# Expert weights of a mixture-of-experts layer loaded as whole rows (16 KB in one piece), both column halves of a matrix together

## The reference

```python
SEQ, D_MODEL, N_EXPERTS, TOP_K, D_FF_2 = 256, 1024, 32, 4, 1024
# each of 256 tokens goes to 4 of 32 experts, y is the normed input of 256 x 1024
g = y @ w_gate_2[e] + b_gate_2[e]          # 1024 x 1024 for each expert
u = y @ w_up_2[e] + b_up_2[e]              # 1024 x 1024
g = minimum(g, 7.0); u = clip(u, -7.0, 7.0)
h = (u + 1) * g * sigmoid(1.702 * g)
out[token] += gate[token, e] * (h @ w_down_2[e] + b_down_2[e])   # 1024 x 1024
```

## Time and profile before

| | |
|---|---|
| median of 3 runs | 2488.28 us (2487.64 to 2488.79) |
| the profiled execution | 2488.91 us, of which the trace spans 2487.1 us |
| PE busy | 2242.4 us (90%) |
| PEld, DVE, ACT, POOL busy | 1451.0, 859.0, 568.9, 28.4 us |
| DMA | 594.04 MB, 239 GB/s on average over the span |
| chain that ended last, by engine | PE 66%, DMA 13%, SP's queue 10%, DVE 5%, issue 3%, ACT 2% |
| mean granted clock of TensorE | 0.955 of full speed |

### The profile page before, as it was taken

The page is one execution under the profiler, slowest core; times in us unless marked ns, Lnnn a source line. Parts: engine busy times, 40 slices in busy tenths (PEclk is TensorE's granted clock), DMA queues, the critical chain, the costliest instruction groups (busy, mean ns, idle before and its releaser), DMA issues.

```text
span 2487.1 us, 27199 instructions
## 1 busy us (share of the span) xinstructions
PE 2242.4 (90%) x11674; PEld 1451.0 (58%) x11674; DVE 859.0 (35%) x1503; ACT 568.9 (23%) x938; POOL 28.4 (1%) x61
## 2 busy tenths in 40 slices
PE   6998999998999999999998899888988898888981
PEld 3776878786875689998878433333333333333330
DVE  4244443523846667543655311111011111111101
ACT  3223332422424355433434200000000000000000
POOL 0000000000002100000000000000000000000000
PEclk8999999999999999999999899999999999999996
DMA  9533443324214445454206699999999999999990
GB/s 330 193 112 102 135 155 117 104 93 159 93 51 162 161 137 196 151 185 169 82 35 234 219 387 387 386 387 387 387 387 387 387 387 387 387 387 386 386 360 22
DMA packets 328288, 594.04 MB, mean 239 GB/s; under 512 B 6256, under 2 KB 78064, under 8 KB 327504
## 3 DMA queue, kind: packets, MB, share of 16 engines
q1 hardware_dynamic: 326240, 589.66, 65.7%
q10 hardware_dynamic: 1904, 2.31, 0.3%
HBM read 590.90 MB, written 1.05 MB: 238 GB/s over the span
## 4 chain that ended last, share of the span: by engine, by line
PE 66%; DMA 13%; SPq 10%; DVE 5%; issue 3%; ACT 2%; POOL 0%; DVEq 0%; ACTq 0%; POOLq 0%
PE ps L864 13%; PE ps L268 12%; PE ps L270 12%; PE ps L269 12%; DMA ring<-in_w_up_dram 12%; SPq L2019 10%; PE ps L835 2%; PE ps L852 2%; DVE wr L974 2%; PE ps L339 1%; PE ps L594 1%; PE ps L573 1%; PE ps L888 1%; DMA ring<-in_even_w_in_dram 1%; PE ps L580 1%
## 5 line engine op out<-in xcount | busy, mean ns | idle before, releaser
L864 PE MATMUL ps<-ring,big 128*64 128x512 f32 x3072 | 717.3, 623 | 108.1 <-DMA ring<-in_w_up_dram 66.1
L864 PEld LDWEIGHTS ps<-ring,big 128*64 128x64 f32 x3072 | 249.7, 143 | 550.1 <-issue 549.8
L268 PE MATMUL ps<-h_hi,wr 128*128 128x512 f32 (+1 forms) x960 | 341.8, 356 | 29.5 <-DVE h_lo L1026 25.3
L269 PE MATMUL ps<-h_lo,wr 128*128 128x512 f32 (+1 forms) x960 | 333.8, 348 | 0.0
L270 PE MATMUL ps<-h_hi,wr 128*128 128x512 f32 (+1 forms) x960 | 333.5, 347 | 0.0
L974 DVE TENSOR_TENSOR wr<-ring,wr 128x1024 fp32r<-128x1024 f32 (+1 forms) x248 | 283.7, 1203 | 132.9 <-ACT wr L1561 132.8
L1561 ACT CAST wr<-ring 128x1024 fp32r<-128x1024 f32 (+1 forms) x248 | 238.5, 1031 | 124.0 <-PE ps L270 101.5
L268 PEld LDWEIGHTS ps<-h_hi,wr 128*128 128x128 f32 x960 | 185.5, 193 | 61.5 <-issue 35.0
L269 PEld LDWEIGHTS ps<-h_lo,wr 128*128 128x128 f32 x960 | 185.6, 193 | 23.5 <-issue 2.9
L270 PEld LDWEIGHTS ps<-h_hi,wr 128*128 128x128 f32 x960 | 185.3, 193 | 21.8
L1435 DVE TENSOR_SCALAR hT<-ps 128x512 f32<-128x512 f32 x32 | 22.1, 692 | 334.9 <-PE ps L888 334.9
(11 more groups left out here) (288 smaller groups left out, 2616.8 us busy)
## 6 DMA issues: line engine op xcount, KB each, us to landing
ring<-in_w_gate_dram SPq DMA_DIRECT2D x64, 2048.0 KB, 19.7
ring<-in_w_up_dram SPq DMA_DIRECT2D x64, 2048.0 KB, 19.8
ring<-in_w_down_dram SPq DMA_DIRECT2D x64, 2048.0 KB, 19.9
ring<-in_ada_w_dram SPq DMA_DIRECT2D x24, 2048.0 KB, 10.9
ring<-in_ffn_w_up_dram SPq DMA_DIRECT2D x44, 1024.0 KB, 7.5
ring<-in_ffn_w_down_dram SPq DMA_DIRECT2D x16, 1408.0 KB, 6.1
ring<-in_w_in_dram SPq DMA_DIRECT2D x9, 2048.0 KB, 7.8
ring<-in_odd_w_qkv_dram SPq DMA_DIRECT2D x6, 2048.0 KB, 8.3
```

What stands on the lines that cost most here:

```text
L268: e.matmul(o, l[0], r[0], start=first, stop=False)
L269: e.matmul(o, l[0], r[1], start=False, stop=False)
L864: ins = e.matmul(pt[HALF[z], :], lhs[:, k, HALF[z]], wt[:, k, :], start=k == 0, stop=False, skip_group_check=True)
```

## The change

All 1024 columns of a matrix row are loaded together. Row 8p + k of a matrix goes to partition p, place k (`"(p k) n -> p (k n)"`), so that a partition's share of a load, four rows, is one piece of 16 KB. A load is still 2 MB and still half of one matrix of one expert, now the half k = 0 to 3 or k = 4 to 7 for every partition. Since the contraction index on partition p is now 8p + k and no longer 128k + p, the features of the other operand are permuted with it: `eighth(v, k)` takes every eighth column of `yN` or of the hidden activations, 128 of them 32 bytes apart, as the stationary operand.

`both` now fills two banks at once, and the couple is of k = 0 to 3 or k = 4 to 7 with both column halves. A pair does gate for both halves, two biases, up for both halves, two biases, then scatter, gather, both transposes, and down. Gate and up use the banks 4, 5 and 6, 7 in turn (`banks_of`). DVE multiplies sigmoid and gate in `gated` while up's matmuls run, and copies the first turned half; ACT copies the second. ACT's copy of the turned gates stands behind its copy of the output.

```diff
-    gu = [view(hflat, 1536 * i, 3, 512) for i in range(2)]
+    hid = view(hflat, 0, 3, D)
...
+    def eighth(v, k):
+
+        return v.rearrange("p (q k) -> p k q", k=KC)[:, k, :]
...
+        def banks_of(b):
+
+            return ((4, 5), (6, 7)) if b % 2 == 0 else ((6, 7), (4, 5))
...
+                        ins = e.matmul(pt[:, P * c:P * c + P], eighth(yN[:, n, :], 4 * hf + c), Sx[b % 2][:, 0, n, :],
...
-        def both(pt, lhs, u, ready):
-
-            for z in range(2):
-                e.wait_ge(s_w[(u + z) % 7], 16 * ((u + z) // 7 + 1))
-            ready()
+        def both(pts, lhs, u, first):
+
             for k in range(KC):
-                for z in range(2):
-                    wt = view(ring, SLOT * XS[(u + z) % 7], KC, 512)
-                    ins = e.matmul(pt[HALF[z], :], lhs[:, k, HALF[z]], wt[:, k, :], start=k == 0, stop=False,
-                                   skip_group_check=True)
-                    if k == KC - 1:
-                        ins.then_inc(s_wused[(u + z) % 7])
+                v = u + 2 * (k // 4)
+                if k % 4 == 0:
+                    for z in range(2):
+                        e.wait_ge(s_w[(v + z) % 7], 16 * ((v + z) // 7 + 1))
+                for hf in range(2):
+                    for z in range(2):
+                        wt = view(ring, SLOT * XS[(v + z) % 7], 4, D)
+                        ins = e.matmul(pts[hf][HALF[z], :], lhs[:, k, HALF[z]], wt[:, k % 4, 512 * hf:512 * hf + 512],
+                                       start=k == 0, stop=False, skip_group_check=True)
+                        if k % 4 == 3 and hf == 1:
+                            ins.then_inc(s_wused[(v + z) % 7])
+                    if k == KC - 1 and hf == 0 and first:
+                        ins.then_inc(fullsem(first))
 
         def pair(b, E, nxt):
             u = 12 * b
-            for hf in range(2):
-                for v, bias in enumerate((bgr, bur)):
-                    name = ("gu"[v], b, hf)
-                    pt = take(e, name, bank=4 + 2 * hf + v)
-
-                    def ready():
-                        if hf == v == 0:
-                            e.wait_ge(*emptied(("xt", b, 0)))
-                            e.wait_ge(*emptied(("xt", b, 1)))
-                    both(pt, XT[b % 2], u + 4 * hf + 2 * v, ready)
-                    if hf == v == 0:
-                        if b < NE // 2:
-                            e.wait_ge(s_E, b + 1)
-                        else:
-                            e.wait_ge(s_ovs, b - NE // 2 + 1)
-                    if b == hf == 0:
-                        e.wait_ge(s_late[v], 16)
-                    e.matmul(pt[:, :], E, bias[:, 512 * hf:512 * hf + 512], start=False, stop=False,
-                             skip_group_check=True).then_inc(fullsem(name))
-
-            def turn(hf):
-                pt = take(e, ("ht", b, hf), bank=4 + hf)
-                e.wait_ge(s_h, 2 * b + hf + 1)
-                for c in range(4):
-                    ins = e.transpose(pt[:, P * c:P * c + P], gu[hf][:, 1, P * c:P * c + P], ident)
-                ins.then_inc(fullsem(("ht", b, hf)))
-
-            turn(0)
+            G, U = banks_of(b)
+            for v, bias in enumerate((bgr, bur)):
+                names = [("gu"[v], b, hf) for hf in range(2)]
+                pts = [take(e, names[hf], bank=(G, U)[v][hf]) for hf in range(2)]
+                if v == 0:
+                    e.wait_ge(*emptied(("xt", b, 0)))
+                    e.wait_ge(*emptied(("xt", b, 1)))
+                both(pts, XT[b % 2], u + 4 * v, None)
+                if v == 0:
+                    if b < NE // 2:
+                        e.wait_ge(s_E, b + 1)
+                    else:
+                        e.wait_ge(s_ovs, b - NE // 2 + 1)
+                if b == 0:
+                    e.wait_ge(s_late[v], 16)
+                for hf in range(2):
+                    e.matmul(pts[hf][:, :], E, bias[:, 512 * hf:512 * hf + 512], start=False, stop=False,
+                             skip_group_check=True).then_inc(fullsem(names[hf]))
             if 0 < b < NE // 2:
                 scatter(b - 1)
             if nxt:
-                gather(b + 1)
-            turn(1)
-            for n in range(2):
-                last = u + 9 + 2 * n
-                pt = take(e, ("y", b, n), bank=4 + n, by=(s_wused[last % 7], last // 7 + 1))
-
-                def ready():
-                    if n == 0:
-                        e.wait_ge(*emptied(("ht", b, 0)))
-                        e.wait_ge(*emptied(("ht", b, 1)))
-                both(pt, HT[b % 2], u + 8 + 2 * n, ready)
-                if n == 0 and nxt:
-                    turn_gates(b + 1)
+                gather(b + 1, G)
+            for hf in range(2):
+                pt = take(e, ("ht", b, hf), bank=U[hf])
+                if hf == 0:
+                    e.wait_ge(s_h, 2 * b + 2)
+                for c in range(4):
+                    ins = e.transpose(pt[:, P * c:P * c + P], eighth(hid[:, 1, :], 4 * hf + c), ident)
+                ins.then_inc(fullsem(("ht", b, hf)))
+            last = u + 11
+            pts = [take(e, ("y", b, 0), bank=G[0]),
+                   take(e, ("y", b, 1), bank=G[1], by=(s_wused[last % 7], last // 7 + 1))]
+            e.wait_ge(*emptied(("ht", b, 0)))
+            e.wait_ge(*emptied(("ht", b, 1)))
+            both(pts, HT[b % 2], u + 8, ("y", b, 0))
+            if nxt:
+                turn_gates(b + 1, U[0])
 
...
+        def gates(b):
+            for hf in range(2):
+                if b and hf == 0:
+                    e.wait_ge(*filled(("ht", b - 1, 1)))
+                e.wait_ge(*filled(("g", b, hf)))
+                e.tensor_scalar(hid[:, 0, 512 * hf:512 * hf + 512], bank(("g", b, hf))[:, :], 7.0, None,
+                                MIN).then_inc(freesem(("g", b, hf)), 1)
+
+        def gated(b):
+            for hf in range(2):
+                g, sig = (hid[:, i, 512 * hf:512 * hf + 512] for i in (0, 2))
+                e.wait_ge(s_sigm, 2 * b + hf + 1)
+                gate_at[hf] = mark(e.tensor_tensor(sig, sig, g, MULT))
+
+        def hidden(b):
+            for hf in range(2):
+                u, sig = (hid[:, i, 512 * hf:512 * hf + 512] for i in (1, 2))
+                e.wait_ge(*filled(("u", b, hf)))
+                e.tensor_scalar(u, bank(("u", b, hf))[:, :], 7.0, -7.0, MIN, MAX).then_inc(freesem(("u", b, hf)), 1)
+                e.wait_ge(*emptied(("u", b, hf)))
+                e.wait_ge(*gate_at[hf])
+                e.scalar_tensor_tensor(u, u, 1.0, sig, ADD, MULT).then_inc(s_h, 1)
+
+        gate_at = {}
+
+        def hidden_turned(b):
+            e.wait_ge(*filled(("ht", b, 0)))
+            e.tensor_copy(HT[b % 2][:, 0:4, :], bank(("ht", b, 0))[:, :].rearrange("p (c s) -> p c s", c=4)).then_inc(
+                freesem(("ht", b, 0)), 1)
 
...
-            hidden(b, 0)
+            gates(b)
             if b + 1 < NE // 2:
                 chosen(b + 1)
-            hidden(b, 1)
+            gated(b)
+            hidden(b)
             if b + 1 < NE // 2:
                 gathered(b + 1)
+            hidden_turned(b)
             expert_out(b)
             if b == 0:
...
-            hidden_turned(b, 0)
             if b + 1 < NE // 2:
                 gathered(b + 1)
-            hidden_turned(b, 1)
+            hidden_turned(b)
+            expert_out(b)
             if b + 1 < NE // 2:
                 gates_turned(b + 1)
-            expert_out(b)
...
-            return ((wg, wu)[r // 2 % 2], r % 2, r // 4) if r < 8 else (wd, r % 2, (r - 8) // 2)
+            return (wg, wu, wd)[r // 4], r % 2, r // 2 % 2
 
         def expert(u):
             src, z, hf = of_load(u % 12)
             if u >= 7:
                 e.wait_ge(s_wused[u % 7], u // 7)
-            e.dma_start(view(ring, SLOT * XS[u % 7], KC, 512), src[2 * (u // 12) + z].rearrange(
-                "(k p) n -> p k n", p=P)[:, :, 512 * hf:512 * hf + 512]).then_inc(s_w[u % 7], 16)
+            e.dma_start(view(ring, SLOT * XS[u % 7], SLOT), src[2 * (u // 12) + z].rearrange(
+                "(p k) n -> p (k n)", k=KC)[:, SLOT * hf:SLOT * hf + SLOT]).then_inc(s_w[u % 7], 16)
 
```

More of the change, by code:

```diff
@@ L820, in pe, with gather @@
         e.matmul(pt[:, NE:2 * NE], tri, Mt[:, 1, :], start=False, stop=True).then_inc(fullsem(("pos", 0)))
-        def gather(b):
+        def banks_of(b):
+            return ((4, 5), (6, 7)) if b % 2 == 0 else ((6, 7), (4, 5))
+        def gather(b, at):
             for hf in range(2):
-                pt = take(e, ("xt", b, hf), bank=6 + hf)
+                pt = take(e, ("xt", b, hf), bank=at[hf])
                 if hf == 0:
@@ L832, in gather, with turn_gates @@
                 for c in range(4):
-                    d = 4 * hf + c
                     for n in range(2):
-                        ins = e.matmul(pt[:, P * c:P * c + P], yN[:, n, P * d:P * d + P], Sx[b % 2][:, 0, n, :],
```

(30 more changed lines are left out.)

13 lines of the change are left out of this document (removed).

## The result

The changed kernel takes 2417.16 us in the median of 4 runs (2415.76 to 2417.57), the kernel before 2488.53 us (2487.64 to 2489.18). The ratio is 0.9712, with a 95% interval from 0.9696 to 0.9729: 71 us or 2.9% faster. The profiled execution spans 2415.8 us. The range of 2386 to 2440 holds the time, but only because it takes in rival 1 (2410 to 2435), in whose lower third the time lies. The forecast itself, 2396 us, is 21 us too low, and its own range of 2386 to 2404 misses by 13 us.

The account below looks back on a forecast made before the run. Transfers were taken to bound the experts' stage: -98 us for faster loads, +5 at the ring's start and +1 at the end sum to -92, so 2396 us. The range was 2386 to 2440 us, its own range 2386 to 2404.

Parts of the forecast that it names:

- rival 1: Gather and hidden transposes: operands spaced 32 bytes slow PE, up to 4.8 us a pair; 2410 to 2435 us, chance 0.26.
- The bound before and the closing sum: Experts' stage: transfers bound it; 185 loads end to end at 5.42 us each make 1003 us.
- slack of 9.3 us: Experts' stage before the change: PE could go 9.3 us a pair faster (55.7 us) than the loads allow (65.0 us).
- The size of the piece: Expert loads: 16 KB pieces instead of 2 KB raise 387 to 429 GB/s, 4.89 us a load, -98 us.
- Rivals 2, 3 and 4: Expert loads stay at 387 GB/s, 2489 us (0.07); reach 408, 2439 us (0.07); fall to 370, 2534 us (0.05).
- The ring at the start: Start of the experts' stage: ring full, PE sets the pace, transfers stand idle until 1477 us; +4 to +5 us.
- The work of PE: Experts' pairs: instruction counts unchanged; a pair without late loads costs 55.7 + 0.8 = 56.5 us, hidden behind loads.
- slack of 2.2 us: Experts' stage after the change: PE's 56.5 us a pair against 58.7 us of loads leaves 2.2 us.
- new wait: End of each pair: PE waits for ACT's copies of output and gates, 0.8 us a pair, costing nothing within the slack.
- The DVE row: A spaced DVE reduction against an adjacent one, used to price spaced weight loads: 0.6 ns an element, 3.1 us for 40 instructions.
- 15 x 0.9 us: Lower end of rival 1's cost: PE exceeds the loads by 0.9 to 2.6 us in each of 15 pairs.
- Covers that held: Transposes behind gather: scatter (3.44 us) and gather (3.59 us) hide DVE's 2.8 us of clamps and products; no cost.

Follow-up runs that it names:

- e1: The changed kernel, but gather reads 128 adjacent columns of yN, not every eighth (features in wrong order, only time read): 2401.19 us.
- e4: The changed kernel with four pieces of 4 KB per partition, rows unpermuted and all operands adjacent: 2439.33 us.
- e5: The changed kernel with two rows in a piece (8 KB) and operands of every second column, 8 bytes apart: 2413.01 us.
- e2: The changed kernel, but the transposes of the hidden activations read adjacent columns (wrong rows met, only time read): 2416.61 us.
- e8: The changed kernel with the next gates transposed between the two down couples and their copy ahead of the output's on ACT: 2410.81 us.
- e6: The changed kernel with four adjacent rows in a 16 KB piece and operands of every fourth column, 16 bytes apart: 2416.49 us.

## Why the prediction was right or wrong

**The bound before and the closing sum: right.** 185 loads end to end explained the stage, and they do so again in e1: 185 x (5.42 - 4.90) us = 96 us, less the pauses of 6 us below, is 90 us, for 89 us measured between the medians. One reading was loose: of the slack of 9.3 us, "The waits make 7.3 us of it" counts 0.8 us of ACT's wait that the pair of 55.7 us has too; the waits for loads make 6.5 us.

**The size of the piece: right, with one rate misread and some luck in the one taken.** I took 429 GB/s for the stream; where nothing disturbs it, it is 428 (e1). The order of the sizes is now measured on long streams: 387 GB/s at 2 KB, 409 at 4 KB (e4), 421 at 8 KB (e5), 428 at 16 KB (e1). Per piece and engine that is 84.7, 160, 311 and 612 ns, which is a line: 9.3 ns for each piece and 36.8 ns for each 1000 bytes (37.7 ns for each KB). So "it is almost gone at 4 KB" was wrong: spread over the bytes, half of what 2 KB pay is left there. The 426 GB/s of a short burst misled me, and with it the bound of 4.92 us; the value taken came from a burst of 10 KB pieces, for which the line gives 424 GB/s. That burst read about 1% too fast and pieces of 16 KB are about 1% faster than those of 10 KB; the two errors cancelled, which was luck. The rule of 3 cycles in the Trainium skill (DMA: Bandwidth & Descriptors, Why small descriptors are slow), weighed in the prediction at 4.1%, is too small: from 2 to 16 KB these runs show 10.6%. Rivals 2, 3 and 4 are refuted: the rate is neither 387 nor 408 nor lower.

**The ring at the start: right for adjacent operands.** In e1 the transfers pause once for long, some 4 us before 1480 us, and briefly at 1515 to 1525 (slices of 5 us from 1400 us on):

```profile
...
GB/s 3 0 0 318 433 429 436 423 433 426 429 436 419 423 416 72 403 426 433 433 439 419 429 351 370 446 423 426 429 436 433 423 423 429 423 436 433 419 433 426
...
```

Together 5 to 6 us, where 4 to 5 were forecast. In the changed kernel itself gather's extra time comes on top, and there are two long pauses and some short ones:

```profile
...
GB/s 0 0 0 66 439 423 429 426 433 436 429 282 374 439 439 423 36 390 433 426 436 426 426 439 351 56 400 433 433 423 436 429 426 429 426 436 423 347 419 419
...
```

**The work of PE: this step failed**, at "The number of matmuls, bias, scatter, gather and transposes is as before" and the sum of 56.5 us that came from it. The number is as before, but gather's instructions went from 112 to 234 ns each, +3.9 us a pair, more than the slack of 2.2 us, so PE and not the transfers bound the kernel. The signs that the prediction gave for rival 1 are all there: a rate of 423 GB/s at 16 KB, 0.2 us of waits for loads, 7.49 us for gather. 56.5 and 3.9 us would make 60.4 us a pair; it takes 59.58, since the rest is shorter than forecast. In e1, pair 2 takes 55.6 us, new wait included (1526.69 to 1582.32 us, shown below); the gate and up couples with their biases, for one, take 31.7 us where they took 32.3. The upper bound of rival 1 had this right for gather (+3.6) and wrong for the transposes, which cost nothing measurable (e2, and 0.90 us in the chain). The DVE row that I took as the nearest, 0.6 ns an element, gave 77 ns a load; the loads grew by 143 ns, the pace of the instructions by 122 ns. I had the rival with its price and its threshold, and gave it a quarter where it was the case: when the price's bounds (0 to 4.8 us) lie around a slack of 2.2 us, the central forecast should not assume the lower one.

What the rival then cost is spread otherwise than its 15 x 0.9 us. The chain views give the starts of pairs 3 and 4 and the end of the last down couple, where the last scatter starts; first the changed kernel, then e1, where pair 2 starts too (1536.10 us in the view above):

```profile
...
1595.68 13.95 PE ps L873 x64
...
1655.24 13.95 PE ps L873 x64
...
2362.05 3.63 PE ps L859 x8
...
```

```profile
...
1526.69 13.95 PE ps L873 x64
...
1582.32 7.09 PE ps L873 x31
...
1638.93 7.09 PE ps L873 x31
...
2343.78 3.63 PE ps L859 x8
...
```

Pairs 2, 3 and 4 start 9.4, 13.4 and 16.3 us later than in e1 (1.3 us of it lie ahead of the first gather), and the last couple ends 18.3 us later. So nine tenths of the loss are there after four pairs: as long as the ring holds loads, PE sets the pace with adjacent columns too, and a slow gather costs its 3.9 us in full or nearly so. The twelve pairs that follow, PE at 59.6 us against 58.8 us of loads, add 2 us: some 5 us up to pair 15, of which 3 us come back because e1 waits there for its last loads. The medians of the two kernels are 16.0 us apart, the profiled executions 18.2 us. The rival's sum charged all pairs alike and so had 14 us; the rest of the way from its 2410 us to 2417 is in the base, which was 5 us low (see the end of this section).

**The new wait: right**, 0.9 us for 0.8; taking it away shortens the pair by 0.7 us (e8). "Costs nothing, as long as that slack lasts": the slack did not last, and e8 shows 6 us of it.

**Covers that held:** DVE's clamps and products stay hidden behind scatter and gather, no wait of PE for them is among its waits in the middle stretch, of which the three lines shown with the result are all.

With adjacent columns the forecast of 2396 would have met 2401. The five microseconds are about 2 of rate (428 for 429, 4.90 us for 4.89, over 185 loads), 1 at the start of the stage, and 2 of the session, in which the kernel before took 2490.3 us and not 2488.3.

## What to carry to other kernels

A stage that is bound by transfers gains from larger pieces, by a fixed cost per piece that can be read off two long streams of different piece size. Work out beforehand what the next bound is, to the microsecond per round, and price every instruction whose operand changes its layout against that slack, not only those whose number changes. Where a buffer is full at the start, the first rounds have no slack: there such a price is paid in full. When a permutation is needed, put it where it is done once, in the copy that writes the buffer, and not where each round reads it; or choose one that leaves two neighbours together.

## What the runs showed of the hardware that I had not expected

- A float32 weight load of 128 columns takes 192 ns with adjacent columns, 196 ns with 8 bytes from one to the next, 329 ns with 16 and 335 ns with 32 (gather in e1, e5, e6 and the change). In gather, matmuls of 128 columns stand 112 ns apart with the first and 234 ns apart with the last.
- In the transposes the same 32 bytes lengthen a weight load from 141 to 192 ns (e2) and change nothing in the time, 2416.61 for 2417.16 us. Why they pay so much less than gather's was not tried.
- A transfer's piece costs 9.3 ns beside its bytes at each of the four sizes from 2 to 16 KB, on streams of 660 us and more; the burst of 2 us with 4 KB pieces read 4% above the stream (426 for 409 GB/s).
- PE at 97% busy held a granted clock of 1.00 over 660 us, where with 6.5 us of waits for loads a pair it had 0.96 and, in e1, with 2.4 us a pair 0.99.
